# A streamed two-layer trunk on one core: layer norms in two token halves, a ring of three weight buffers, block loops written out

## What is computed

```python
h = swiglu(x * (1.0 + scale[:, 0]) + shift[:, 0], w_ff_in[l, 0], w_ff_out[l, 0])
x = layer_norm(DEEP_ALPHA * x + 0.5 * gate[:, 0] * h, ln_g[l, 0], ln_b[l, 0])
u = x * (1.0 + scale[:, 1]) + shift[:, 1]
...
x = layer_norm(DEEP_ALPHA * x + gate[:, 1] * h, ln_g[l, 1], ln_b[l, 1])
h = swiglu(x * (1.0 + scale[:, 2]) + shift[:, 2], w_ff_in[l, 1], w_ff_out[l, 1])
x = layer_norm(DEEP_ALPHA * x + 0.5 * gate[:, 2] * h, ln_g[l, 2], ln_b[l, 2])
```

## Time and profile before

| | before |
|---|---|
| median of three runs | 2906.2 us (2902.56, 2906.2, 2915.89) |
| profiled execution: span, 43873 instructions | 2909.0 us |
| PE busy | 2595.3 us (89%) |
| DVE busy | 1532.1 us (53%) |
| ACT busy | 710.0 us (24%) |
| POOL busy | 88.0 us (3%) |
| HBM traffic | 86 GB/s over the span |

### The profile page before, as it was taken

One profiled execution on the slowest core, in us unless ns is written; L12 is line 12 of the kernel. 1 busy time (PEld: TensorE's weight loads), 2 busy tenths in 40 slices (PEclk: granted clock), 3 DMA queues, 4 the chain that ended last, 5 costly groups with the idle time before them and its releaser, 6 DMA issues.

```text
span 2909.0 us, 43873 instructions
## 1 busy us (share of the span) xinstructions
PE 2595.3 (89%) x18258; PEld 2481.8 (85%) x18258; DVE 1532.1 (53%) x2371; ACT 710.0 (24%) x784; POOL 88.0 (3%) x116
## 2 busy tenths in 40 slices
PE   5999998986779788999999799999667897999996
PEld 5999997984668557999999799999567796999996
DVE  4768665634542434665574676335888345333333
ACT  2122123333111422321112422113312213221222
POOL 0000000100000000100000100000000001000000
PEclk9999999996885789999999899999779898999998
DMA  6445432130000111243343143222100021222211
GB/s 262 159 148 200 172 118 85 61 76 0 1 1 4 53 44 58 102 166 118 123 155 117 69 164 108 94 81 73 66 1 1 16 73 44 81 71 94 84 57 51
DMA packets 39568, 250.89 MB, mean 86 GB/s; under 512 B 5312, under 2 KB 5888, under 8 KB 15792
## 3 DMA queue, kind: packets, MB, share of 16 engines
q1 hardware_dynamic: 26784, 172.25, 17.2%
q0 software_dynamic: 11248, 73.97, 7.5%
q10 hardware_dynamic: 1440, 3.32, 0.3%
HBM read 246.09 MB, written 3.43 MB: 86 GB/s over the span
## 4 chain that ended last, share of the span: by engine, by line
PE 58%; DVE 10%; ACT 1%; issue 1%; POOL 0%; DMA 0%; DVEq 0%; ACTq 0%
PE ps L272 49%; PE ps L432 2%; PE ps L411 1%; PE ps L1946 1%; DVE x L516 1%; DVE tb L1709 1%; DVE be L1709 1%; DVE ln_rstd L512 1%; PE ps L1164 1%; DVE wm L1709 1%; PE ps L1153 1%; PE ps L1161 1%; PE ps L1334 1%; DVE uf L469 1%; DVE ta L1709 1%
## 5 line engine op out<-in xcount | busy, mean ns | idle before, releaser
L272 PE MATMUL ps<-u_hi,w_hi 128*128 128x288 f32 x3392 | 735.2, 299 | 75.5 <-POOL u_lo L481 46.5
L272 PE MATMUL ps<-u_lo,w_hi 128*128 128x288 f32 x3392 | 732.9, 298 | 0.0
L272 PE MATMUL ps<-u_hi,w_lo 128*128 128x288 f32 x3392 | 732.4, 298 | 0.0
L272 PEld LDWEIGHTS ps<-u_hi,w_hi 128*128 128x128 f32 x3392 | 553.2, 191 | 79.3 <-issue 77.2
L272 PEld LDWEIGHTS ps<-u_lo,w_hi 128*128 128x128 f32 x3392 | 553.3, 191 | 0.0
L272 PEld LDWEIGHTS ps<-u_hi,w_lo 128*128 128x128 f32 x3392 | 553.1, 191 | 0.0
L247 DVE TENSOR_TENSOR w_lo<-w_raw,w_hi 128x2048 fp32r<-128x2048 f32 x176 | 403.2, 2292 | 224.1 <-ACT w_hi L242 223.6
L242 ACT ACTIVATE w_hi<-w_raw 128x2048 fp32r<-128x2048 f32 x176 | 337.0, 1915 | 549.8 <-PE ps L272 519.3
L540 DVE SCALAR_TENSOR_TENSOR ada_out<-ada_w,c_act 128x1024 f32<-128x1024 f32 x272 | 317.0, 1221 | 43.1 <-DMA ada_w<-in_w_ada 26.3
L272 PE MATMUL ps<-h_lo,w_hi 128*128 128x288 f32 x1600 | 338.2, 296 | 0.0
L272 PE MATMUL ps<-h_hi,w_hi 128*128 128x288 f32 x1472 | 321.1, 300 | 5.0 <-DVE h_lo L1709 5.0
(11 more groups left out here) (346 smaller groups left out, 2120.8 us busy)
## 6 DMA issues: line engine op xcount, KB each, us to landing
w_raw<-in_w_in SPq DMA_DIRECT2D x88, 1024.0 KB, 4.9
ada_w<-in_w_ada POOLq DMA_DIRECT2D x64, 1024.0 KB, 5.0
w_raw<-in_w_out SPq DMA_DIRECT2D x32, 768.0 KB, 4.1
w_raw<-in_w_out SPq DMA_DIRECT2D x32, 640.0 KB, 3.8
w_raw<-in_w_mix_in SPq DMA_DIRECT2D x10, 1024.0 KB, 4.9
ada_w<-in_w_ada SPq DMA_DIRECT2D x8, 1024.0 KB, 25.9
w_raw<-in_w_mix_out SPq DMA_DIRECT2D x4, 1024.0 KB, 4.7
w_raw<-in_w_glu SPq DMA_DIRECT2D x4, 1024.0 KB, 4.7
```

The source lines that it names most:

```text
L272: m = pe.matmul(out[:, a, :], w, mv[:, a, :], start=start and n_ == 0, stop=stop and n_ == 2)
```

## The change

Weights: three buffers of each kind, `w_lo` written over `w_raw`; SP loads block g when the product of block g-3 is done; both splits of block g+2 stand ahead of the wait for the product of block g, and take the block's own width. All block loops are written out. The output products of the mixer and of S5 become eight blocks of one tile (they were four of two), with the mean matmuls between them as in the feed-forwards.

Norms: the chain runs twice, over columns 0 to 287 (a = 0) and 288 to 575 (a = 1). All `u_lo` go to POOL, in tiles of 288. `head` lets block 0 wait, per tile, for the second half's `u_lo`. The last S5 parameter stage moves behind LN3, and y is stored per half.

```diff
-          + feed_forward_blocks(2) + (("glu", 4), ("s5_out", 4)) + feed_forward_blocks(3))
...
+          + feed_forward_blocks(2) + (("glu", 4), ("s5_out", KD)) + feed_forward_blocks(3))
...
+    w_raw = rw("w_raw", [P, NS, BLOCK])
+    w_lo = nc.alloc_sbuf_tensor_at("w_lo", [P, NS, BLOCK], F32R, offset=W0)
+    w_hi = rw("w_hi", [P, NS, BLOCK], F32R)
...
+        for b in range(dict(STREAM)[name]):
+            g = first[name] + b
+            if g >= NS:
+                sp.wait_ge(s_blk, g - NS + 1)
+            sp.dma_start(w_raw[:, g % NS, 0:WIDTH[g]], src(b)).then_inc(s_raw[g % NS], 16)
...
+        act.activation(w_hi[:, g % NS, 0:WIDTH[g]], w_raw[:, g % NS, 0:WIDTH[g]], ACT.Copy).then_inc(s_whi, 1)
...
+        dve.tensor_tensor(w_lo[:, g % NS, 0:WIDTH[g]], w_raw[:, g % NS, 0:WIDTH[g]],
+                          w_hi[:, g % NS, 0:WIDTH[g]].bitcast(F32), ALU.subtract).then_inc(s_wlo, 1)
...
+    def head(pe, name, n):
+
+        if n:
+            for a in range(2):
+                late_mean(pe, n - 1, a)
+                square_sums(pe, n - 1, a)
+        for b in range(2):
+            def ready(k):
+                wait_u_half(pe, n, 1, k)
+            product(pe, name, b, 2, KD, u_hi, u_lo, ready if b == 0 else None)
...
+    def out_tensor(pe, name, n, kk, mov_hi, mov_lo, ready=None):
+
+        for b in range(KD - 2):
+            if b >= 2:
+                pe.wait_ge(s_evac, first[name] + b - 1)
+                mean_tile(pe, b - 2, 0)
+                mean_tile(pe, b - 2, 1)
+            product(pe, name, b, 1, kk, mov_hi, mov_lo, ready if b == 0 else None)
+        tail(pe, name, n, kk, mov_hi, mov_lo)
...
+            for b in range(n):
+                split_hi(act, g0 + b + 2)
+                act.wait_ge(s_blk, g0 + b + 1)
+                act.activation(halves(sg[:, b % 2, :]), pair(2 * (b % 2)), ACT.Silu).then_inc(s_sg, 1)
...
+            for b in range(KD if s == 0 else KD - 2):
+                split_hi(act, g1 + b + 2)
+                if b in stages:
+                    stages[b]()
...
+        ln_scalar(act, f"out{f}1", (0, 2, 3, 5)[f])
+        if f == 2:
+            stages[6]()
...
+        for b in range(KD - 2):
+            split_lo(dve, g1 + b + 2)
+            residual(dve, name, n, b)
+            if b < len(stages):
+                stages[b]()
+        ln_vector(dve, name, n)
+        if stages:
+            stages[6]()
...
+    def late_mean(pe, n, a):
+
+        if a == 0:
+            pe.wait_ge(s_ra, 2 * n + 2)
+        else:
+            pe.wait_ge(s_evac, done(LN_NAMES[n]))
+        for k in range(KD - 2, KD):
+            m = mean_tile(pe, k, a)
+        m.then_inc(s_mean, 1)
...
+            split_hi(act, g_next + a)
+            for k in range(KD):
+                act.wait_ge(s_cen, ln_count(n, a, k))
+                if a or k >= SQ:
+                    act.wait_ge(s_var, ln_count(n, a, k) - SQ)
+                act.activation(sq[:, k % SQ, :], half(x, k, a), ACT.Square).then_inc(s_sq, 1)
+            act.wait_ge(s_var, ln_count(n, a, KD - 1))
+            act.activation(ln_std[:, a, :], pair(3)[:, a, :], ACT.Sqrt, bias=cols[:, C_EPS:C_EPS + 1]).then_inc(s_std, 1)
+            if n < NMOD - 1:
+                u_scalar(act, n + 1, a)
+                continue
...
+        for a in range(2):
+            for k in range(KD):
+                pool.wait_ge(s_uhi, ln_count(nth(n), a, k))
+                pool.tensor_tensor(half(u_lo, k, a), half(u_f32, k, a), half(u_hi, k, a).bitcast(F32),
+                                   ALU.subtract).then_inc(s_up, 1)
...
+    def wait_u_half(eng, n, a, k):
+
+        eng.wait_ge(s_up, ln_count(nth(n), a, k))
...
+        dve.wait_ge(s_blk, first[name] + KD - 1)
+        residual_part(dve, n, KD - 2, 0, HALF, 0).then_inc(s_ra, 1)
+        split_lo(dve, g_next)
+        dve.wait_ge(s_blk, first[name] + KD)
+        residual_part(dve, n, KD - 1, 0, HALF, 0).then_inc(s_ra, 1)
+        for a in range(2):
+            if a:
+                for b in range(KD - 2, KD):
+                    dve.wait_ge(s_blk, first[name] + b + 1)
+                    residual_second_half(dve, n, b)
+            dve.wait_ge(s_mean, 2 * n + a + 1)
+            for k in range(KD):
+                dve.tensor_tensor(half(x, k, a), half(x, k, a), pair(1)[:, a, :], ALU.subtract).then_inc(s_cen, 1)
+            if a:
+                split_lo(dve, g_next + 1)
+            dve.wait_ge(s_std, 2 * n + a + 1)
+            chains["dve"].step(dve.reciprocal(ln_rstd[:, a, :], ln_std[:, a, :]))
+            dve.wait_ge(s_sq, ln_count(n, a, KD - 1))
+            dve.wait_ge(s_cen, ln_count(n, a, KD - 1))
+            for k in range(KD):
+                dve.tensor_tensor(half(x, k, a), half(x, k, a), ln_rstd[:, a, :], ALU.mult).then_inc(s_nrm, 1)
+                if a and n < NMOD - 1 and k:
+                    u_sample(dve, n + 1, k - 1)
         if n == NMOD - 1:
             return
```

More of the change, by code:

```diff
@@ L184, in trunk @@
     s_mod1 = sem("second_modulation_row_summed")
[L185 removed]
+    s_raw = [sem(f"weight_block_loaded_{n}") for n in range(NS)]
     s_whi = sem("weight_hi_ready")
@@ L239, in split_hi @@
[L239 to L265, removed]
+    WIDTH = []
@@ L273, in three @@
         return m
[L275 to L299, removed]
@@ new lines, in weights, with tile_of, product @@
+    def weights(g, tiles, kk):
+        return [w[:, g % NS, 0:kk * tiles * P].rearrange("p (k m c) -> p k m c", k=kk, m=tiles) for w in (w_hi, w_lo)]
+    def tile_of(t):
+        return t if callable(t) else (lambda k: t[:, k, :])
+    def product(pe, name, b, tiles, kk, mov_hi, mov_lo, ready=None):
+        g, hi, lo = first[name] + b, tile_of(mov_hi), tile_of(mov_lo)
+        wh, wl = weights(g, tiles, kk)
+        pe.wait_ge(s_wlo, g + 1)
+        if g >= 2:
+            pe.wait_ge(s_evac, g - 1)
+        for m_ in range(tiles):
+            for k in range(kk):
+                if ready is not None and m_ == 0:
+                    ready(k)
+                mm = three(pe, pair(2 * (b % 2) + m_), wh[:, k, m_, :], wl[:, k, m_, :],
+                           halves(hi(k)), halves(lo(k)), k == 0, k == kk - 1)
+        mm.then_inc(s_blk, 1)
@@ L364, in ffn_vector @@
             if s == 0:
-                gate_vector(dve, (0, 2, 3, 5)[f])
-            residual_vector(dve, f"out{f}{s}", (0, 2, 3, 5)[f], 1)
-    s5_link = []
-    def residual_vector(dve, name, site, tiles):
-        g1, count = first[name], dict(STREAM)[name]
-        ends_sublayer = name[-1] != "0"
+                gate_vector(dve, site)
+                for b in range(KD):
+                    split_lo(dve, first[f"out{f}0"] + b + 2)
+                    residual(dve, f"out{f}0", site, b)
+                    if f == 0:
+                        ada_unit(dve, SEGS[0][1], b // 2, b % 2)
@@ L1457, in mix_tensor @@
     def mix_tensor(pe):
-        body, count = product(pe, "mix_in", 2, KD, u_hi, u_lo, ready_first=u_ready(pe, 1))
-        blocks_loop(pe, count, body, start=1)
+        head(pe, "mix_in", 1)
+        for b in range(2, 10):
+            product(pe, "mix_in", b, 2, KD, u_hi, u_lo)
         norms_tensor(pe)
@@ L1465, in mix_tensor, with out_scalar @@
         pe.wait_ge(s_ol, 9)
-        body, count = product(pe, "mix_out", 2, KD, u_hi, u_lo)
-        blocks_loop(pe, count, body)
-    def out_scalar(act, name):
-        g0 = first[name]
-        def body(i, r, _):
-            act.wait_ge(s_blk, g0 + r + 1 + 2 * i)
-            split_hi(act, g0 + 2, r, i)
-        blocks_loop(act, 4, body)
+        out_tensor(pe, "mix_out", 1, KD, u_hi, u_lo)
+    def out_scalar(act, name, n):
+        for b in range(KD - 2):
+            split_hi(act, first[name] + b + 2)
+            if n == 1 and b == 2:
+                conditioning_scalar(act, s_in2, True)
+        ln_scalar(act, name, n)
     def mix_scalar(act):
```

436 lines of the change are left out of this document (180 added, 256 removed).

## The result

The changed kernel takes 2936.3 us (median of four runs, 2935.1 to 2938.1), the kernel before 2906.7; the ratio is 1.0094, with a 95% interval from 1.0076 to 1.0113. Slower by 0.9%, as forecast in sign; the forecast was 2927, the range 2905 to 2948. The profiled executions have spans of 2935.5 and 2909.0, and the following goes by them.

What follows compares the result with a forecast made beforehand. The prediction took PE's matmuls to bound the steady blocks, with losses where PE stands still at norms. Its terms summed to +20.5 us on a span of 2909.0, giving a median of 2927 us, range 2905 to 2948.

Steps and rivals of the forecast that it cites:

- First matmul at 32.1 us: At a norm boundary, block 0's first matmul comes 32.1 us after the last residual's start, where it was at 22.9.
- End of block 0 at 48.0: At a norm boundary, the next block 0 ends 48.0 us after the last residual's start; in LN0 it was 42.1.
- A pair of modulation and `u_hi` 1.0: On ACT, modulation and `u_hi` of one 288-column tile cost 1.0 us together, eight tiles 8.0.
- Second sums 7.0 at the low clock: On PE, half 1's eight sums of squares take 7.0 us, since the pause lowers the clock.
- First rival: Clock holds through ACT's eight modulations, half 1's sums cost 3.8 instead of 7.0: 2908, no change to tell; chance 0.25.
- A half on POOL 1.0: On POOL, a low part of 288 columns takes 1.0 us, half of the 1.97 for 576.
- Second rival: A half on POOL costs as much as a whole, 1.97: +7.3 in five places, so 2964; chance 0.08.
- Delta rule -5.7: Ahead of the delta rule, the splits standing earlier save 5.7 us of PE's 7.6.
- Stage: At LN3 and S5, the parameter stage leaves the residual's path (-5.3) and stands uncovered ahead of S5's matrices (+8.9); together +7.5.
- Loops and ring at nothing: Written-out loops and the ring of three weight buffers cost nothing; an output block takes 8.96 looped, 8.95 written out.
- Only behind that stand the squares of half 1: On ACT, half 1's squares wait behind half 0's eight modulations (17.8 us) and a 1.9 us weight split, until 19.7.
- the span's sum: The place-by-place total of all gains and losses, +20.5 us against a span of 2909.0.

Runs made afterwards that it cites:

- e2_whole: The changed kernel with norms over all 576 columns instead of halves, its other edits kept: 2902.2 us, ratio 0.9969 to the kernel before.
- e3_squares_first: The changed kernel with both halves centred, squared and summed before half 0's modulations: 2900.6 us, ratio 0.9969 to the kernel before.
- e6_warm_norms: The changed kernel with idle matmuls on PE around the sums in LN0, LN1, LN2 and LN4: 2926.9 us, ratio 1.0045 to the kernel before.
- e1_unrolled: The kernel before with its three loops written out, nothing else: 2914.3 us, ratio 1.0023 to the kernel before.
- e9_split_late: The changed kernel with a boundary's second weight split moved behind half 1's squares (ACT) and last sample (DVE): 2940.7 us, ratio 1.0103 to the kernel before.
- e10_means_first: e7_squares_first_warm with the second split late, both means ahead of the first sums, and 18 instead of 26 idle matmuls: 2880.0 us, ratio 0.9904 to the kernel before.
- e5_warm_attention: The changed kernel with nine idle matmuls on PE ahead of the attention's first scores: 2931.2 us, ratio 1.0060 to the kernel before.
- e7_squares_first_warm: e3_squares_first with nine idle matmuls ahead of the attention and 26 behind the sums of four norms: 2896.7 us, ratio 0.9961 to the kernel before.

## Why the prediction was right, and where it was not

The sign and its cause held: the halves run one behind the other, and PE, which is the bound, waits for the second; without halves (e2_whole) or with another order (e3_squares_first) the loss is gone. The chain's figures were measured as follows.

- First matmul at 32.1 us (its terms sum to 32.0): 31.8, 31.8, 32.4 and 34.1. In the last, LN4, half 0's sums already fell into the lower clock and took 5.84 instead of 4.15. End of block 0 at 48.0: 47.0 to 48.8.
- A pair of modulation and `u_hi` 1.0: 0.99 from start to start. The 0.411 for 288 columns was read from an operation that reads `ps`; `u_hi`, which doesn't, took 0.44.
- Second sums 7.0 at the low clock: 6.68, and 4.04 with PE kept busy (e6_warm_norms). First rival, a clock that holds: not so.
- A half on POOL 1.0: 0.80 beside an idle DVE, 0.87 in the mean of LN2. Second rival, no shrinking: not so. The row answers to the one in the earlier trace rows:

```profile
L514 POOL TENSOR_TENSOR u_lo<-u_f,u_hi 128x288 fp32r<-128x288 f32 x16 | 13.7, 865 | 87.1 <-ACT u_hi L493 86.8
```

- Delta rule -5.7: -5.5. ACT's squares follow the evacuation directly:

```profile
653.15 0.64 ACT L824 ACTIVATE misc<-ps 128x576 f32<-128x576 f32 x1
653.88 0.68 ACT L875 ACTIVATE sqm<-qkv 128x576 f32<-128x576 f32 x1
```

- Stage: no gap ahead of LN3's residual, 8.9 us of stage ahead of `be`, as worked out; S5 gave a little of it back, +4.7 instead of +7.5.
- Loops and ring at nothing: the blocks' lengths and the absence of `w_lo` in the waits bear it out. At no cost is not quite right for the loops, since e1_unrolled lost 0.23%, with its clock low in every execution.

One step failed though the sum came out: "Only behind that stand the squares of half 1, although DVE has long centred it", with 1.9 us for the weight split on ACT. In LN2 DVE began to centre half 1 only at 1629.46, behind eight scalings that ran beside POOL and behind the residuals and mean of half 1, 0.2 us ahead of ACT's split. So DVE's queue alone kept half 1 back until 1.5 us before ACT was free for its squares, and that two queues gave nearly the same time is chance: the time came out although only one of them was in the chain. Moving the split alone won 0.7 to 1.0 us of the first matmul (e9_split_late). Moving half 1 ahead on ACT and DVE won 36 us (e3_squares_first), and with PE's means, the late split and the idle matmuls 56 in all (e10_means_first, 8.7 of them in the attention by the profiles).

One term was missing: the attention's +7.4 us. It is clock, not work, and is more than the 6 us by which the span's sum was short (26.5 against 20.5); the other rows together came 1.4 below theirs. The range was wide enough for a term that the forecast did not have; that part is luck. Writing out the loops alone already brings 4.4 of it, and the kernel before has executions at the same low mean clock (e1_unrolled): it hangs on something other than the norms. What decides when the clock rises in the attention stays open: it took 73.7 to 82.4 us in the one profile of each of twelve kernels with the same instructions there. With PE kept busy ahead of it, it took 81.1, 81.1, 78.0 and 73.7, and without 75.0 to 82.4.

## What to carry to other kernels

Cutting a serial chain into two halves pays only if the second half runs under the first; look for that on every engine's list, since one queue that puts all of half 0 ahead of half 1 (here ACT's modulations, DVE's scalings and PE's sums alike) makes the halves add up. Mending one of these queues moves the wait to the next: here two together (ACT and DVE) brought most of the gain, and left a wait of 3.1 us for the third. And a change that leaves a stage alone can still alter its time through the clock: compare a stage's PE time at equal work before giving the difference to an edit.

## What the runs showed of the hardware that was not expected

- The same 236 records of the attention took PE 61.7 to 73.2 us by the granted clock alone, with the work of DVE and ACT equal to 0.03 us.
- A block of 96 matmuls takes 12.80 us throughout in nine of the twelve profiled executions. In that of e2_whole the blocks of the first feed-forward and the mixer's input blocks took 12.48 each, at a granted clock of 1.00 and with the same traffic; in that of e5_warm_attention it was the second and the fourth feed-forward, in that of e7_squares_first_warm the mixer's input blocks alone. One such block:

```profile
340.00:352.48 12.48, 12.48 (x98) 12.48 (x98) 8.85 (x15) 2.50 (x3) 0.53 (x1) 1.00 0.48 169
```

  Over one feed-forward that is about 9 us, so single executions of these kernels can differ by it; what sets the pace, no run here shows.
- Eight DVE scalings of 288 columns took 3.04 us in a row while POOL was idle (0.45 each, overlapping; e10_means_first) and 4.83 in LN2 after the change. There five took 0.45 as well; the other three each began some 0.1 us behind one of POOL's low parts, took 1.05, and ended 0.3 us behind it.
- PE's clock can stay at the lower level while PE works: in the attention after the change for 47.5 us with PE busy for 43.1 of them.
